# Copying the dilated caches in five pieces of 61,184-byte rows in place of four pieces of 65,504-byte rows

## The reference

```python
ext_k = jnp.concatenate([cache_dil_k[layer], kb_s], axis=1)
ext_v = jnp.concatenate([cache_dil_v[layer], vb_s], axis=1)
...
dk_s.append(ext_k[:, DEC_SEQ:]); dv_s.append(ext_v[:, DEC_SEQ:])
```

## Time and profile before

| | |
|---|---|
| median of 3 runs | 1212.7 us (1204.87 to 1214.85) |
| the profiled execution's own time | 1214.5 us |
| its span, first to last instruction | 1212.8 us |
| TensorE busy | 919.1 us (76%) |
| VectorE busy | 634.5 us (52%) |
| POOL busy | 416.6 us (34%) |
| DMA, mean over the span | 397 GB/s, 481.20 MB moved |
| of the chain that ended last | DMA 43%, PE 34%, issue 9% |
| copies | 64 transfers, 1023.5 KB each |

### The profile page before, as it was taken

The page is one execution under the profiler, slowest core; times in us unless marked ns, Lnnn a source line. Parts: engine busy times, 40 slices in busy tenths (PEclk is TensorE's granted clock), DMA queues, the critical chain, the costliest instruction groups (busy, mean ns, idle before and its releaser), DMA issues.

```text
span 1212.8 us, 13466 instructions
## 1 busy us (share of the span) xinstructions
PE 919.1 (76%) x3662; PEld 422.9 (35%) x3662; DVE 634.5 (52%) x1601; ACT 352.2 (29%) x959; POOL 416.6 (34%) x432
## 2 busy tenths in 40 slices
PE   2797998487547979954778877887588778777784
PEld 0343336343113448831223332333233323333231
DVE  3200102426525425123776777777777777777745
ACT  0000005432102012221333333323433444244323
POOL 1101333123310001111555445545455445554541
PEclk9799999778978979986998989989998999999986
DMA  9999999999988899999999999999989999999996
GB/s 367 422 390 375 399 413 398 410 374 364 414 350 259 297 363 388 371 404 376 427 427 407 427 426 427 427 427 427 427 368 427 427 427 428 428 428 427 427 427 274
DMA packets 72857, 481.20 MB, mean 397 GB/s; under 512 B 9985, under 2 KB 10338, under 8 KB 27378
## 3 DMA queue, kind: packets, MB, share of 16 engines
q0 software_dynamic: 54784, 377.55, 75.8%
q1 hardware_dynamic: 18034, 103.15, 22.3%
HBM read 477.41 MB, written 70.32 MB: 452 GB/s over the span
## 4 chain that ended last, share of the span: by engine, by line
DMA 43%; PE 34%; issue 9%; DVE 5%; ACT 4%; POOL 3%; POOLq 1%; SPq 1%; DVEq 0%; ACTq 0%
DMA R<-in_uv,idst 28%; PE ps L929 11%; PE ps L550 7%; DMA R<-in_sb_v,vrow 5%; DMA R<-in_wts 5%; PE ps L880 5%; POOL R L454 2%; PE ps L576 2%; PE ps L835 2%; DMA vrow<-in_vrow 2%; DVE R L1705 2%; DMA R<-in_sb_k 1%; DMA R<-in_uv,idec 1%; PE ps L702 1%; PE ps L518 1%
## 5 line engine op out<-in xcount | busy, mean ns | idle before, releaser
L929 PE MATMUL ps<-R,diag 128*128 128x512 f32 x1024 | 501.4, 641 | 162.3 <-ACT diag L1203 162.0
L454 POOL DMA_INDIRECT R<-in_uv,idst x256 | 307.6, 1202 | 375.5 <-PE ps L929 302.5
L1705 DVE CUSTOM_DVE_ANT_0 R<-R,H 128x1024 f32<-128x1024 f32 x264 | 319.4, 1224 | 204.7 <-DMA R<-in_uv,idst 195.4
L929 PEld LDWEIGHTS ps<-R,diag 128*128 128x128 f32 x1024 | 200.4, 203 | 463.3 <-ACT diag L1203 243.0
L1181 ACT ACTIVATE gel<-dots 128x2 f32<-128x2 f32 x132 | 26.8, 203 | 407.7 <-DVE dots L1705 407.7
L550 PE MATMUL ps<-R,HT 128*128 128x512 f32 x192 | 94.5, 632 | 4.5 <-DMA R<-in_wts 4.5
L402 POOL DMA_DIRECT2D R<-in_wts x36 | 19.3, 539 | 220.9 <-PE ps L835 80.2
L1203 ACT ACTIVATE diag<-const,wgt 128x128 f32<-128x128 f32 x256 | 88.7, 393 | 13.7 <-ACT wgt L1184 1.5
L702 PE MATMUL ps<-R,ast 128*32 128x512 f32 x256 | 38.4, 689 | 36.7 <-DMA R<-in_sb_v,vrow 36.1
L1184 ACT ACTIVATE wgt<-gel,gst 128x1 f32<-128x1 f32 x264 | 63.3, 287 | 4.3
L880 PE MATMUL ps<-HT,R 128*128 128x264 f32 x256 | 61.2, 400 | 1.9 <-DMA R<-in_wts 1.9
(11 more groups left out here) (274 smaller groups left out, 819.1 us busy)
## 6 DMA issues: line engine op xcount, KB each, us to landing
R<-in_wts POOLq DMA_DIRECT2D x48, 1024.0 KB, 12.4
out_dil_k_s<-in_dil_k SPq DMA_DIRECT2D x32, 1023.5 KB
out_dil_v_s<-in_dil_v SPq DMA_DIRECT2D x32, 1023.5 KB, 8.4
R<-in_sb_k SPq DMA_DIRECT2D x64, 256.0 KB, 7.6
R<-in_sb_k POOLq DMA_DIRECT2D x64, 256.0 KB, 6.2
m_all<-in_win_k SPq DMA_DIRECT2D x8, 512.0 KB
R<-in_win_v SPq DMA_DIRECT2D x8, 512.0 KB
R<-in_uv,idst POOLq DMA_INDIRECT x256, 11.8
```

What stands on the lines that cost most here:

```text
L454: pool.indirect_dma_start(out=R[:, row_slot(k), :], out_offset=None, in_=A["uv"], in_offset=bass.IndirectOffsetOnAxis(ap=idst[:, par, k:k ...
L929: last = pe.matmul(ps[:, banks + q, :], diag[:, k % 4, :], R[:, row_slot(k), D + q * 512:D + (q + 1) * 512], start=False, stop=False, skip ...
L1705: dve.tensor_tensor_reduce(u, u, H[:, t, :], 1.0, 0.0, ALU.mult, ALU.add, dots[:, k:k + 1]).then_inc(s["dot_done"], 1)
```

## The change

The rows of a piece become 15,296 numbers (61,184 B) in place of 16,376 (65,504 B); a piece is still 16 rows. Four such pieces hold 3,915,776 B, and a fifth holds what is left of the 4,192,256 B: 16 rows of 4,320 numbers (17,280 B), 276,480 B in all. The same rule of waiting holds, with 5 pieces for each sample and cache. The first part of sample 2's copy, between the window rows, stays two pieces; three in place of two come later. There are 80 copies in place of 64.

```diff
--- before.py
+++ after.py
@@ -39,6 +39,8 @@
 KVS = 8
 CPB = NPG // KVP
 VQ = NPG // 4
+COPY = 16 * 15296
+COPIES = -(-(PAST - 1) * DG // COPY)
 TOPK = 16
 NKEY = 128
 QUAD = 32
@@ -321,15 +323,15 @@
 
 
                 src, dst = ((A["dil_k"], A["dil_k_s"]), (A["dil_v"], A["dil_v_s"]))[m]
-                n = (PAST - 1) * DG // 4
+                at, n = q * COPY, min(COPY, (PAST - 1) * DG - q * COPY)
                 landed = copied[2 * odd + m]
                 if not (isinstance(pair, int) and isinstance(q, int) and pair + q == 0):
-                    sp.wait_ge(landed, pair * 64 + q * 16)
-                sp.dma_start(dst[bass.ds(pair * 2 + odd, 1), bass.ds(q * n, n)].rearrange("a (r n) -> (a r) n", r=P),
-                             src[bass.ds(pair * 2 + odd, 1), bass.ds(q * n + DG, n)].rearrange("a (r n) -> (a r) n", r=P)
+                    sp.wait_ge(landed, (pair * COPIES + q) * 16)
+                sp.dma_start(dst[bass.ds(pair * 2 + odd, 1), bass.ds(at, n)].rearrange("a (r n) -> (a r) n", r=P),
+                             src[bass.ds(pair * 2 + odd, 1), bass.ds(at + DG, n)].rearrange("a (r n) -> (a r) n", r=P)
                              ).then_inc(landed, 16)
 
-            def copy_windows(pair, odd, quarters=range(4)):
+            def copy_windows(pair, odd, quarters=range(COPIES)):
                 for q in quarters:
                     for m in range(2):
                         copy_piece(pair, odd, m, q)
@@ -370,7 +372,7 @@
                 window_rows(sp, DV, b, b % 6, A["win_v"], A["dil_v_s"], dv_ready)
             sp.wait_ge(s["vd_used"], 3)
             sp.dma_start(subk, A["subk"].rearrange("p (g n) -> p g n", g=16)).then_inc(s["subk_in"], 16)
-            copy_windows(1, 0, range(2, 4))
+            copy_windows(1, 0, range(2, COPIES))
             for pair, odd in ((1, 1), (2, 0), (2, 1), (3, 0), (3, 1)):
                 copy_windows(pair, odd)
 
@@ -385,7 +387,7 @@
             sp.wait_ge(s["kv_out"], 16 * 12)
             sp.wait_ge(s["new_out"], 64)
             for n in range(4):
-                sp.wait_ge(copied[n], 16 * 4 * NB // 2)
+                sp.wait_ge(copied[n], 16 * COPIES * NB // 2)
             sp.wait_ge(s["y_out"], 16 * (2 + QUADS))
```

## The result

The changed kernel took 1221.09 us (median of 17 runs, 1216.4 to 1226.23) against 1213.62 us for the kernel before (17 runs in the same rounds, 1204.87 to 1218.88). The ratio is 1.0069, 95% interval 1.0053 to 1.0085: slower by about 8 us, clear of the noise though under 1%. The forecast was 1218.8. The profiled execution of the changed kernel took 1226.2 us (span 1224.5), 5 us more than its median, so its rows show more than the typical loss.

The account below looks back on a forecast made before the run. DMA engines were taken as full from about 432 us, TensorE from 119 to 198 us behind a key-page wait. Terms 4.5 + 0 + 1.6 + 0 = +6.1 us on the median 1212.7 gave 1218.8 us, range 1198 to 1229.

Parts of the forecast that it names:

- Bytes and issue cost: All copies: same 67 MB copied, and 16 more issues at about 0.5 us each mostly fall into waits; 0.
- Term 1: Sample 1's first key pages, queued behind the copies: SP released later, pages land faster; +4.5 us at 118.92 (-2.6 to +7.4).
- by steps: Pricing SP's later release at the key pages by the extra waiting steps of samples 0 and 1: +9.8 us.
- by bytes: Pricing SP's later release at the key pages by bytes that must land first, at 0.267 MB per us: +5.7 us.
- The second stretch at the low clock: After TensorE's wait for key pages, longer idling might keep the clock low: 2.5 us, in the upper bound only.
- Term 2: Sample 2's first two pieces, 210 to 250 us: -0.7 us from fewer bytes, +0.7 behind 382 us; 0.
- Term 3: Copies alone, 396 to 432 us: one change of sample leaves more empty DMA time; +1.6 us (0 to 4).
- Term 4: 432 to 575 us: gaps at five more changes of sample are filled from POOL's queue; 0, or +9 us uncovered.
- Better rows: Rival, windows with copies: rows 61,184 B apart end a memory slowdown, gaining 14 us (7 to 23), 1205 us; chance 0.30.
- the rate of the windows with copies rises by more than 3%: Sign in the windows with copies that would make the prediction wrong.
- Nothing added: Rival at the key pages: shorter pieces and queue make up for the step, TensorE's stall unchanged, 1214 us; chance 0.12.
- Never covered: Rival at each change of sample: small-piece wait with POOL's queue empty, +22.9 us, 1235 us; chance 0.10.

Follow-up runs that it names:

- e2: Kernel before with only the fourth piece split in two (rows of 48,224 B and 17,280 B) and a wait between: 1217.21 us, ratio 1.0064.
- f1: Changed kernel with the small piece's wait kept for samples 0 and 1, left out for samples 2 to 7: 1216.32 us, ratio 1.0058 to the kernel before.
- g2: Changed kernel with the rest of sample 2 and all of sample 3 issued without waits between pieces: 1213.34 us, ratio 1.0037 to the kernel before.
- e1: Changed kernel with the fifth, small piece issued without waiting, for all samples: 1211.61 us, ratio 1.0019 to the kernel before.
- c1: Only the 64 copies of the kernel before (rows of 65,504 B), no waits, nothing else computed: 209.58 us.
- c2: Only the 80 copies of the changed kernel (rows of 61,184 B), no waits, nothing else computed: 209.78 us.
- f2: Kernel before with no waits in the last piece of sample 2 and in sample 3: 1205.41 us, ratio 0.9943.
- g1: Kernel before with no waits in the last piece of sample 2 and in samples 3 to 7: 1225.12 us, ratio 1.0122.
- e4: Kernel before with sample 1's even key pages issued ahead of its last pair of copies: 1210.16 us, ratio 1.0003.

## Why the prediction was right, step by step

- **Bytes and issue cost, 0.** Right: without waits, 64 and 80 copies take the same 209.6 and 209.8 us.
- **Term 1, +4.5 us.** Right in place, and right in size in part by luck: the runs give 4.0 to 4.7 us, with some 4 us of uncertainty, but both parts of the sum were too small and they cancelled. SP was released 12.1 us later (120.03 for 107.94), where +8 was taken and 10 was the upper bound; e2, f1 and g2 have the same step and give 119.07, 119.87 and 119.53, so this is not that one execution. Pricing by steps (+9.8) was nearer than by bytes (+5.7), in part because the share of the stretch did not stay full, as the byte method assumed (0.92 at 100 to 110 us for 0.95). The second page landed 5.54 us after its issue in place of 9.74, a saving of 4.2 where 3.5 was taken, and 6.3, 6.0 and 5.0 in e2, f1 and g2. TensorE went on 7.9 us later, above the bound of 7.4, in an execution 5 us over its median; in e2, whose profiled execution is its median, it was 4.8. TensorE's longest wait was named as 10 to 11 us; it was 15.0 (12.4 in e2). The second stretch at the low clock did not come: after the wait L578 took 1.94 us at the 1.2 GHz level, as 1.93 before, and then 1.00 again.
- **Term 2, 0.** Nothing contradicts it, and no run took it alone. From the first output of new keys to the first copy behind the sub-keys the profiles give 184.4 us before and 181.6 to 187.1 in the others, more spread than the 0.7 us in question.
- **Term 3, +1.6 us.** The mechanism is shown: the window of the copies alone has 0.77 for 0.87, 3.6 us more idle, inside the bounds. That figure hangs on the cut, for the changed kernel's window opens in the wait for a small piece. From sample 3's first piece to sample 4's it is 30.10 us for 29.43, at 0.81 for 0.85; from the first copy behind the sub-keys to sample 4's it is 49.28 us for 46.44, of which 0.7 us are the 0.28 MB that term 2 moved. The copies alone give 1.8 us a sample, the very price of the forecast, but this is closer than its working: that took packets at the 427 GB/s of loads, and at the 334 of copies a full and a small piece differ by 3.1 - 0.8 = 2.3 us. The whole effect of the later six samples was 1.3 to 2.1 us.
- **Term 4, 0.** The shares from 443 us on are 1.02, 0.99 and 1.00: the cover holds, though the last copy is issued 30 us later. Six samples at 1.8 us would have been 11 us.
- **Sum.** +6.1 us forecast, +8.4 by the ratio (6.4 to 10.3). What is left over is of the size of e1's +0.19%, 2.3 us, whose interval includes zero; it stays open.
- **Better rows** fell: c1 and c2 are equal, and e2 has the loss with the old rows. Copies run at 334 GB/s at full share with either spacing, which fits the lower rate beside copies; that this comes from moving each byte in and out of memory is likely, and no run separates it. The Trainium skill (DMA: Bandwidth & Descriptors, section Latency and other measured facts) names 512 KiB as the smallest spacing at which it saw a loss, and no run here has rows that far apart. One sign had been named wrongly: "the rate of the windows with copies rises by more than 3%" would have been read as met in a window fixed at 396 to 432 us, where the changed kernel has 314 GB/s, because that window begins some 11 us earlier in its stage; cut by stage, the rate falls from 292 to 269.
- **Nothing added** fell with the key pages' 120.03 and with the 0.50% between e1 and the changed kernel.
- **Never covered** was right of the copies alone, where 16 more copies cost 14.7 us, and wrong of the kernel, where the 12 of them in the later six samples cost 1.3 to 2.1 us: there another queue takes the gaps. The Trainium skill (DMA: Bandwidth & Descriptors, section Anatomy of one DMA) gives a fixed cost of about 2 us a transfer, from which the prediction had an estimate of 16 us for 16 more copies, two in flight. The copies alone come near that estimate.

## What to carry to other kernels

A wait between pieces of a background transfer is cheap only where another queue fills the gap and nothing urgent stands behind it in the same list. For what stands behind it, count the waiting steps and not the bytes, and price each by the time from issue to issue in the trace (some 7 us here; two more steps, less what the shorter pieces saved, made 11 to 12 us). Then subtract what the shorter queue gives back to the transfer behind (4 to 6 us here). Where a stretch has idle transfer engines, deepen the queue there (f2, 0.9943), and only there: with the same freedom for the copies that run beside weights, the copies held these back and the kernel lost 1.2% (g1). Releasing an issuing queue earlier gained nothing where the engines were full behind it (e4).

## What the runs showed of the hardware

Copies from DRAM to DRAM reach 332 to 336 GB/s in each direction on 16 engines at full share (c1, c2), against 427 GB/s for the gathers. The page of c1, the run with the old rows and no waits:

```profile
DMA packets 2049, 67.08 MB, mean 323 GB/s; under 512 B 1025, under 2 KB 1025, under 8 KB 1025
```

Of 2,049 packets half are over 8 KB, 1,024 for 64 copies of 16 rows: a row of 65,504 B goes as one packet. That fits what g1 showed, a queue of such packets beside which an 8 KB-row weight tile took 49 us to land; that the packet size is the cause was not tested.
